# Block one's feed-forward with the convolved half of its input projection as 512-column matmuls, each half in a bank of its own

## What is computed

```python
def conv_gated_ffn(h, w_up, conv_w, conv_b, w_down):
    S = h.shape[1]
    up = h @ w_up
    a, g = up[..., :D_FF], up[..., D_FF:]
    ap = jnp.pad(a, ((0, 0), (CONV_WIDTH - 1, 0), (0, 0)))
    a = conv_b + sum(conv_w[j] * ap[:, j:j + S] for j in range(CONV_WIDTH))
    return (jax.nn.gelu(a) * g) @ w_down
```

## Time and profile before

| | us |
|---|---|
| median of 3 runs | 2124.91 |
| the three runs | 2124.47, 2124.91, 2125.14 |
| profiled execution | 2125.03 |
| its span | 2123.1 |
| PE busy | 2101.8 (99%) |
| PE weight loads busy | 1909.6 (90%) |
| DVE busy | 1638.7 (77%) |
| ACT busy | 1237.7 (58%) |

### The profile page before, as it was taken

One profiled execution on the slowest core, in us unless ns is written; L12 is line 12 of the kernel. 1 busy time (PEld: TensorE's weight loads), 2 busy tenths in 40 slices (PEclk: granted clock), 3 DMA queues, 4 the chain that ended last, 5 costly groups with the idle time before them and its releaser, 6 DMA issues.

```text
span 2123.1 us, 39160 instructions
## 1 busy us (share of the span) xinstructions
PE 2101.8 (99%) x16336; PEld 1909.6 (90%) x16336; DVE 1638.7 (77%) x2517; ACT 1237.7 (58%) x2014; POOL 13.1 (1%) x20
## 2 busy tenths in 40 slices
PE   8999999999999999999999999999999999999999
PEld 6898999999998999998888989888898888998888
DVE  7899789888887788877886656887688764778876
ACT  4765656545755756555655447665575644766554
POOL 0000000000000000000000000000000000000000
PEclk9999999999999999999999999999999999999999
DMA  9565557667645467555555644555555556345553
GB/s 371 196 220 209 182 211 256 242 235 281 221 156 179 156 221 234 200 183 188 185 193 186 230 152 149 201 189 192 187 184 189 189 205 203 139 169 207 189 189 130
DMA packets 122098, 424.55 MB, mean 200 GB/s; under 512 B 13457, under 2 KB 22033, under 8 KB 121154
## 3 DMA queue, kind: packets, MB, share of 16 engines
q1 hardware_dynamic: 121922, 422.06, 57.1%
HBM read 417.68 MB, written 4.33 MB: 199 GB/s over the span
## 4 chain that ended last, share of the span: by engine, by line
PE 90%; DVE 4%; ACT 4%; DMA 1%; issue 1%; POOL 0%; SPq 0%; ACTq 0%; DVEq 0%
PE bank L207 89%; ACT arena L259 2%; DVE arena L214 1%; DVE lo L214 1%; DMA raw<-W 1%; ACT hi L259 1%; DVE arena L222 1%; PE bank L211 1%; ACT L259 0%; DVE ada L231 0%; DMA xT<-x 0%; DVE m L214 0%; ACT L251 0%; ACT ych L259 0%; POOL arena L214 0%
## 5 line engine op out<-in xcount | busy, mean ns | idle before, releaser
L207 PE MATMUL bank<-h,hi 128*128 128x256 f32 (+1 forms) x5216 | 1177.5, 312 | 0.0
L259 ACT ACTIVATE hi<-raw 128x1024 fp32r<-128x1024 f32 x656 | 689.2, 1057 | 546.8 <-PE bank L207 483.9
L207 PE MATMUL bank<-h,lo 128*128 128x256 f32 x3312 | 945.7, 286 | 0.1
L207 PEld LDWEIGHTS bank<-h,hi 128*128 128x128 f32 x5216 | 856.4, 190 | 60.9 <-issue 2.6
L214 DVE TENSOR_TENSOR lo<-raw,hi 128x1024 fp32r<-128x1024 f32 x656 | 792.2, 1220 | 91.7 <-ACT hi L259 90.7
L207 PEld LDWEIGHTS bank<-h,lo 128*128 128x128 f32 x3312 | 630.6, 190 | 12.3 <-issue 8.1
L207 PE MATMUL bank<-act,hi 128*128 128x512 f32 x1056 | 370.0, 393 | 0.0
L207 PE MATMUL bank<-act,lo 128*128 128x256 f32 x1056 | 294.7, 279 | 0.0
L207 PEld LDWEIGHTS bank<-act,hi 128*128 128x128 f32 x1056 | 197.9, 187 | 47.3
L207 PEld LDWEIGHTS bank<-act,lo 128*128 128x128 f32 x1056 | 197.9, 187 | 0.0
L259 ACT ACTIVATE arena<-arena 128x256 f32<-128x256 f32 (+4 forms) x202 | 98.6, 494 | 158.7 <-DVE arena L214 151.3
(11 more groups left out here) (155 smaller groups left out, 1983.3 us busy)
## 6 DMA issues: line engine op xcount, KB each, us to landing
raw<-W SPq DMA_DIRECT2D x664, 512.0 KB, 3.5
ada<-WA SPq DMA_DIRECT2D x80, 512.0 KB, 3.6
arena<-WA SPq DMA_DIRECT2D x16, 512.0 KB, 14.1
arena<-conv_rows SPq DMA_DIRECT2D x16, 280.0 KB, 5.9
arena<-taps SPq DMA_DIRECT2D x2, 1792.0 KB, 7.9
p_projected<-arena SPq DMA_DIRECT2D x2, 1024.0 KB, 7.3
arena<-scr SPq DMA_DIRECT2D x16, 128.0 KB, 4.8
arena<-p_projected SPq DMA_DIRECT2D x2, 1024.0 KB, 4.9
```

The source lines that it names most:

```text
L207: return self.done(lambda e: e.matmul(out, l, r, start=start, stop=stop, skip_group_check=True))
L259: return self.done(lambda e: e.activation(out, in_, f, scale=scale, **kw))
```

## The change

The new function `up_in` replaces `first_pairs` and `pair` for block one's input projection. The order of weight tiles stays. The convolved half now has the wide form with a bank of its own, the gate keeps three matmuls of 256 columns and also gets a bank of its own, so a layer takes 44 banks instead of 22. Per m, ACT additionally copies the second share into `ushare`; DVE adds the first share to it and writes the padded tile; and the first tap with its bias moves from DVE to ACT (`Identity` with scale and bias).

```diff
+        ushare = [un(105 + i, 1) for i in range(2)]
...
+            def up_in(l, ms, turns):
+                parts = [(m, part) for m in ms for part in ("conv", "gate")]
+                banks = {}
+                for k, n in turns:
+                    m, part = parts[n]
+                    use = ("up", l, m, part)
+                    if k == 0:
+                        banks[n] = take(WIDE, use)
+                    o = banks[n]
+                    wh, wl, ends = tile([("ffn_w_up", l, k, ("c", m * 128 + (FF if part == "gate" else 0)))])
+                    pe.wait_ge(v_main, ("h", ("n2", l), k))
+                    pe.mm(t256(o, 0), wl, t256(hw, 2 * k), k == 0, False)
+                    if part == "conv":
+                        i = pe.mm(o, wh, t512(hw, k), False, k == KD - 1)
+                    else:
+                        pe.mm(t256(o, 0), wh, t256(hw, 2 * k), False, False)
+                        i = pe.mm(t256(o, 0), wh, t256(hw, 2 * k + 1), False, k == KD - 1)
...
-                    first_pairs(WIDE, [("up", l, m) for m in range(2)], "ffn_w_up", l,
-                                [[("c", m * 128), ("c", FF + m * 128)] for m in range(2)], h_in(("n2", l)))
+                    up_in(l, [0, 1], [(k, n) for k in range(KD) for n in range(4)])
...
-                        pair(WIDE, item, "ffn_w_up", l, [("c", m * 128), ("c", FF + m * 128)], h_in(("n2", l)))
+                        up_in(l, [m], [(k, n) for n in range(2) for k in range(KD)])
```

On DVE, per m:

```diff
+                        v.wait_ge(a_main, ("share", l, m))
+                        v.wait_ge(g_main, ("pads", l))
+                        if m >= 3:
+                            v.wait_ge(v_main, ("conv", l, m - 3))
+                        v.tt(pads[m % 3][:, 2:258], t256(ps(use), 0), ushare[m % 2], ADD).then_inc(v_main, ("pad", l, m), frees=use)
...
-                        v.tt(ftmp[late % 4], ftmp[late % 4], ps(("up", l, late))[:, 256:512], MUL).then_inc(
-                            v_main, ("product", l, late), frees=("up", l, late))
+                        v.wait_ge(pe_main, use)
+                        v.tt(ftmp[late % 4], ftmp[late % 4], t256(ps(use), 0), MUL).then_inc(
+                            v_main, ("product", l, late), frees=use)
...
-                        v.wait_ge(a_main, ("pad", l, m))
-                        v.wait_ge(g_main, ("pads", l))
-                        v.ts(x, pd[:, 2:258], w(2), P("ffn_conv_b", l, m), MUL, ADD).then_inc(v_main)
-                        v.wait_ge(v_main)
+                        v.wait_ge(a_main, ("tap", l, m))
```

On ACT, per m:

```diff
+                        if m >= 2:
+                            a.wait_ge(v_main, ("pad", l, m - 2))
+                        a.wait_ge(pe_main, ("up", l, m, "conv"))
+                        a.act(ushare[m % 2], t256(ps(("up", l, m, "conv")), 1), ACT.Copy).then_inc(a_main, ("share", l, m))
...
-                        a.act(pads[m % 3][:, 2:258], ps(item)[:, 0:256], ACT.Copy).then_inc(a_main, ("pad", l, m))
+                        if m >= 4:
+                            a.wait_ge(v_main, ("act", ("n2", l), m - 4))
+                        a.wait_ge(v_main, ("pad", l, m))
+                        a.act(ftmp[m % 4], pads[m % 3][:, 2:258], ACT.Identity, bias=P("ffn_conv_b", l, m),
+                              scale=P("ffn_conv_w", l, 2 * KF + m)).then_inc(a_main, ("tap", l, m))
```

More of the change, by code:

```diff
@@ L728, in wide @@
                     names = ends + ([use] if k == nk - 1 else [])
+                    if names:
+                        i.then_inc(pe_main, *names)
+                    if ends:
+                        f.tick()
+            def up_in(l, ms, turns):
[15 more added lines that the diff above has]
+                        i = pe.mm(t256(o, 0), wh, t256(hw, 2 * k + 1), False, k == KD - 1)
+                    names = ends + ([use] if k == KD - 1 else [])
                     if names:
@@ L1900, in vector_program @@
                         f.tiles(16)
+                    if m < KF:
+                        use = ("up", l, m, "conv")
+                        v.wait_ge(a_main, ("share", l, m))
[3 more added lines that the diff above has]
+                        v.tt(pads[m % 3][:, 2:258], t256(ps(use), 0), ushare[m % 2], ADD).then_inc(v_main, ("pad", l, m), frees=use)
                     if later is not None:
@@ L1904, in vector_program @@
                     if late is not None:
+                        use = ("up", l, late, "gate")
                         v.wait_ge(a_main, ("gelu", l, late))
-                        v.tt(ftmp[late % 4], ftmp[late % 4], ps(("up", l, late))[:, 256:512], MUL).then_inc(
-                            v_main, ("product", l, late), frees=("up", l, late))
+                        v.wait_ge(pe_main, use)
+                        v.tt(ftmp[late % 4], ftmp[late % 4], t256(ps(use), 0), MUL).then_inc(
+                            v_main, ("product", l, late), frees=use)
                     late = None
@@ L2521, in scalar_program @@
                     if m < KF:
-                        a.wait_ge(pe_main, item)
-                        a.wait_ge(g_main, ("pads", l))
-                        if m >= 3:
-                            a.wait_ge(v_main, ("conv", l, m - 3))
-                        a.act(pads[m % 3][:, 2:258], ps(item)[:, 0:256], ACT.Copy).then_inc(a_main, ("pad", l, m))
+                        if m >= 4:
[3 more added lines that the diff above has]
+                              scale=P("ffn_conv_w", l, 2 * KF + m)).then_inc(a_main, ("tap", l, m))
                         late = m
```

1 line of the change is left out of this document (added).

## The result

| | median, us | runs, us | profiled execution (span) |
|---|---|---|---|
| before, beside it | 2124.69 | 2124.43 to 2125.14, 4 runs | 2125.03 (2123.1) |
| changed | 2143.35 | 2140.1 to 2144.19, 4 runs | 2140.1 (2138.1) |

The ratio is 1.0084 with a 95% interval of 1.0072 to 1.0096: the change costs 18.7 us, where 11.9 were forecast, and the time lies above the range. The profiled execution is the fastest of the four; its span is 15.0 us longer than before.

What follows compares the result with a forecast made beforehand. The prediction took PE, busy 99% of the span, as the bound: 14.9 us of new waiting less 4.7 gained, plus 1.7 for one clock fall, gave 2136.8 us. The range was 2133.9 to 2140.5 us.

Steps and rivals of the forecast that it cites:

- What bounds the kernel, and who owns a bank: Whole kernel: PE, busy 99% of the span, sets the time; the change redistributes who owns a bank when it is wanted.
- the four places named: New PE pauses at up first of layers 0 and 1, block one's second wout and block two's first wo.
- The four stalls: New waits for banks: 6.2 us and 5.1 us at up first, 1.9 us at wout, 1.7 us at wo.
- The elementwise work: Block one's input projection: the changed ACT and DVE work and their new chain cost PE 0 us.
- Rival 5: Input projection: the ACT and DVE exchange becomes the bound, laps 0.3 us longer than PE's; about 2145 us, chance 0.04.
- The gain: Convolved half of the input projection: 352 wide tiles save 13.4 ns each, 4.7 us; 3.5 kept for the range.
- The clock: Behind the long stalls: one fall costs 1.7 us, each stall's part bounded by 0 and twice 1.7; forecast counts one.
- The sum: Whole kernel: 14.9 us of waiting less 4.7 gained, +10.2; 2135.1 us without a clock fall, 2136.8 with one, 2138.5 with two.
- slower cases: Whole kernel: outcomes slower than before by over 4.2 us, given a total chance of 0.96.
- Rival 3: At the long stalls: two clock falls, or one longer than at the start; 2138.5 us, up to 2140.5, chance 0.28.

Runs made afterwards that it cites:

- early: The changed kernel with ScalarE reading the filler's first results ahead of the third h half of norm2: 2130.6 us, ratio 1.002.
- turn: The changed kernel with two banks skipped behind each layer's input projection, so later items find their former banks: 2139.32 us, ratio 1.0063.
- before_tap: The kernel before with only the first tap of the convolution moved to ScalarE: 2125.43 us, ratio 0.9999.
- narrow: early_turn with the convolved half's 512-column matmul split again into two of 256 columns: 2125.68 us, ratio 1.0001.
- gate_wide: early_turn with the gate wide as well, its second share left unread, so the gate lacks one product: 2116.41 us, ratio 0.9958.
- again: The changed kernel run once more without any edit: 2144.4 us.
- warm: The changed kernel with unread matmuls (48 in layer 0, 36 in layer 1) in front of up first's third tile: 2138.97 us, ratio 1.0063.
- full_wide: gate_wide with the gate's second share used: ScalarE copies the bank, GpSimd adds the halves, VectorE multiplies from the sum: 2121.16 us, ratio 0.9983.
- early_turn: The changed kernel with the edits of both early and turn: 2123.43 us, ratio 0.999.
- full_wide_2: full_wide with the last two channel tiles' gates narrow again, multiplied straight from the bank: 2117.99 us, ratio 0.9964.

## Why the prediction was wrong, step by step

- **What bounds the kernel, and who owns a bank: right.** PE stopped at the four places named, released by the engines named, and has no other new pause of over 1 us. early and turn take the pauses away by the causes named.
- **The four stalls, 14.9 us: right but for a misread row.** 6.2 was 6.07, 5.1 was 4.54, 1.9 was 2.0, 1.7 was 1.7; together 14.3. In layer 1 the prediction took 812.82 for the third tile, but that is the second; the third stood at 813.18. With that, its own working gives 817.73 - 813.16 = 4.57 us for this stall. The 0.13 us for the fourth bank did not show in either layer, since the tile before it ran at half pace and the bank was free by its end.
- **The elementwise work, 0: right.** before_tap and narrow both stand level with the kernel before, and no matmul of either stage waits for the low parts. Rival 5 is out.
- **The gain, 4.7 us: mis-sized, 2.65.** This is one of the two steps that failed. The step took the distance of block two's tiles, 346.6 ns, because operand and banks were the same. In block two every tile is wide. Here runs of eight wide tiles alternate with eight narrow ones and stand at 353 to 354. gate_wide shows that the neighbours are the difference, narrow that this is all that the wide form brings. The other end of the range, 3.5 us, was a stage of wide tiles alone too, so neither bound was of the mixed kind. This is 2.05 us of the miss.
- **The clock, 1.7 us for one fall: mis-sized.** This is the other. Each long stall stayed inside its bound of 0 to 3.4 us (2.9 and 1.4 in the first profile), but both paid, in both profiles of the changed kernel, where the forecast let one pay: 4.3 us, 2.6 too little. And the two pauses of some 2 us, which the sum and all rivals had counted as safe, can pay 1.5 us each. The first profile escaped that and again did not: the median lies 3.3 us above the first profile's time, and the larger part of such a difference was the clock's in again, the rest the start's. The prediction noted a granted clock of 1.00 beside half pace in the earlier trace rows. In that trace the first record of the clock stands at 17.48 us, so the 1.00 ahead of it is the lack of a record.
- **The sum.** With the terms as measured it is 14.3 + 4.3 - 2.65 = 15.95 for the first profile, less the 0.85 us of an earlier start: 15.1, and the spans differ by 15.0. Two terms were off by 2.05 and 2.6 us in the same direction; stalls 0.6 us shorter and the earlier start took 1.45 back, which was luck. The median run has 3.3 us more than the profiled one. The range, which ended 15.6 above before, allowed for two falls of the clock, but for none behind the small pauses. (The chances of its slower cases add up to 0.97, where it says 0.96.)

Rival 3, two falls, at 2138.5 and up to 2140.5, had the mechanism of the first profile. Rival 5's number, about 2145, lies nearer to the measured 2143.35, but only by luck: no profile shows its mechanism. The chance of 0.4 for one fall rested on the absence of any long pause in the rows, which is no evidence for either.

The Trainium skill ("TensorE: Matmul & The Clock Gate", HAM oscillation), cited in the prediction, has it that long waits inside a matmul stream throttle the array again each time. For the two long stalls the traces agree, 4 times of 4 (6.8, 3.4, 6.8 and 6.8 us at 0.50). The prediction gave that rule a price, and a chance through rival 3, but not the forecast.

## What to carry to other kernels

A change that takes more banks moves every later take of the pool; list who owned each bank at every first take behind the change, and find the reader that is queued late on its engine. Count each new pause of TensorE of several us twice, once for its length and once for slow matmuls behind it, allow for the second price behind a pause of some 2 us as well, and take the distance of tiles from a stretch with the same mixture of forms, not from one with the same operand. Here moving a few reads ahead and skipping two banks was worth more than the whole wide form.

## What the runs showed of the hardware

**Pauses of PE and the clock behind them**, those over 1.5 us behind the first 100 us of the program, in us from start to start, with the length of the stretch granted 0.50 at that place:

| kernel | up first 0 | 534 to 541 us | down 0 | wout 1 | up first 1 | wo, block two |
|---|---|---|---|---|---|---|
| changed | 6.19: 6.8 | | | 2.13: none | 4.67: 3.4 | 2.42: none |
| again | 6.19: 6.8 | | | 2.14: 3.4 | 4.66: 6.8 | 2.42: 3.4 |
| turn | 6.18: 6.8 | 1.53: none | | | 4.66: 6.8 | |
| early | | 2.19: none | | 2.14: 3.4 | | 2.42: none |
| warm | | | | 2.14: none | | 2.42: 3.4 |
| full_wide | | | 2.31: 3.4 | | | |

The same pause in the same kernel lowers the clock in one execution and not in the next. Of these eleven pauses between 1.5 and 2.4 us five did, of six over 4 us all. All kernels here also pause near 57 us, for 0.5 to 2.2 us, and in seven of the profiles (before 1.90, changed 1.68, again 1.82, before_tap 1.69, narrow 1.85, early_turn and full_wide 2.15) that is over 1.5 us too; none of these lowered the clock, which makes it five of 18. What decides it is not shown. A kernel with pauses spreads (early 6.7 us in seven runs, the changed kernel 4.1 in its first four). Without them narrow spreads by 1.6 us and before_tap by 1.0 in eleven runs each, but early_turn by 4.5 with its clock at 1.000, so the clock is not the only source.

**A wide matmul's price depends on its neighbours**: 347 ns for a tile when all are wide, 353 to 354 when runs of eight alternate with eight narrow tiles, 360 when all are narrow.

**GpSimd and VectorE got into each other's way.** VectorE's subtraction of two operands in SBUF, at 416 ns beside an idle GpSimd, took 614 in the mean with GpSimd's additions beside it, and those took from 0.74 to 1.61 us for the same 128x256. The groups of instructions in full_wide_2 from 330 to 440 us (busy us, mean ns, idle before):

```profile
L214 POOL TENSOR_TENSOR arena<-arena 128x256 f32<-128x256 f32 x19 | 19.2, 1012 | 100.1 <-ACT arena L259 100.1
L214 DVE TENSOR_TENSOR act<-arena,act 128x256 fp32r<-128x256 f32 x18 | 11.1, 614 | 0.0
L214 DVE TENSOR_TENSOR arena<-bank,arena 128x256 f32<-128x256 f32 x20 | 8.4, 418 | 0.0
```

and one such encounter, VectorE, then GpSimd:

```profile
399.75 0.96 DVE L214 TENSOR_TENSOR act<-arena,act 128x256 fp32r<-128x256 f32 x1
...
399.68 0.74 POOL L214 TENSOR_TENSOR arena<-arena 128x256 f32<-128x256 f32 x1 [5.19 <-ACT arena L259]
403.50 1.61 POOL L214 TENSOR_TENSOR arena<-arena 128x256 f32<-128x256 f32 x1 [3.08 <-ACT arena L259]
```

The addition with one operand in a bank took 418 ns, against 423 beside an idle GpSimd. The Trainium skill ("SBUF — State Buffer", SBUF: two separate sides) says that GpSimd and a VectorE operation with two SBUF inputs share a pair of ports, which one holds for its whole instruction while the other is blocked; the rows fit that roughly: the subtraction that began 0.07 us behind GpSimd's addition ended 0.29 us behind it and took 0.54 us more than its usual 0.42. Blocked to the very end of the addition, it would have ended some 0.42 behind it; the profiler's spans on GpSimd are rough. In this kernel it cost no time that the profile shows: the tiles of full_wide_2 stand 347 ns apart as in gate_wide.
